# The Fourier step of a gMLP and Fourier block folded by token t and 256 - t, with a list of overflowing experts split in four and the end of the mixture-of-experts stage rearranged

## What is computed

```python
# first block, second half: mixture of experts on t = norm(x)
scores = sigmoid(t @ w_router); eidx = top 8 of 64 experts (from the 4 best of 8 groups)
routed = sum over chosen e of gate[e] * ((silu(t @ w_eg[e]) * (t @ w_eu[e])) @ w_ed[e])
x = x + gate2 * (routed + shared)

# second block, first layer ("ab"), done once for the tokens x and once for 256 context tokens ctx
z = h @ w_in                                   # h = norm(x) or norm(ctx), 256 x 1024
u, v, g_a, x_b, g_b = split(z)                 # each 512 wide
y_a = u * spatial(layer_norm(v)) * silu(g_a)
xb = x_b.reshape(B, 256, 4, 128)
f = real(fft2(xb, axes=(tokens, channels), norm='ortho'))   # 256 tokens, 4 groups of 128 channels
y_b = f * silu(g_b)
x = x + gate * (concat([y_a, y_b]) @ w_out)
# second layer ("c"): window attention over x with keys and values of ctx, final norm
```

## Time and profile before

| | us |
|---|---|
| median of 3 runs (lowest, highest) | 1126.29 (1125.88, 1126.87) |
| the profiled execution, its own time | 1125.17 |
| its span in the trace | 1123.4 |
| TensorE busy with matmuls | 1079.4 (96%) |
| VectorE, ScalarE, GpSimd busy | 380.8, 277.2, 52.6 |
| bytes moved | 335.48 MB, mean 299 GB/s |
| mean granted clock of TensorE | 0.992 |

### The profile page before, as it was taken

The page is one execution under the profiler, slowest core; times in us unless marked ns, Lnnn a source line. Parts: engine busy times, 40 slices in busy tenths (PEclk is TensorE's granted clock), DMA queues, the critical chain, the costliest instruction groups (busy, mean ns, idle before and its releaser), DMA issues.

```text
span 1123.4 us, 17394 instructions
## 1 busy us (share of the span) xinstructions
PE 1079.4 (96%) x7070; PEld 746.9 (66%) x7070; DVE 380.8 (34%) x974; ACT 277.2 (25%) x619; POOL 52.6 (5%) x85
## 2 busy tenths in 40 slices
PE   6999999999999899999999999999989999999988
PEld 4786776688756465565556655456458888887567
DVE  1298976432722211112111121211332011342941
ACT  2124135501511112112111111102322111212951
POOL 0000202103000000000000000001000001100001
PEclk9999999999999899999999999999999999999999
DMA  9999387945679999999999999999995334210000
GB/s 385 336 421 421 125 346 317 419 186 188 263 311 385 372 422 420 420 408 422 422 419 422 419 422 421 417 422 418 401 410 216 113 113 151 111 38 1 1 1 38
DMA packets 48560, 335.48 MB, mean 299 GB/s; under 512 B 5440, under 2 KB 6816, under 8 KB 8672
## 3 DMA queue, kind: packets, MB, share of 16 engines
q1 hardware_dynamic: 46080, 329.01, 71.9%
q10 hardware_dynamic: 2176, 3.37, 1.0%
q0 software_dynamic: 224, 1.97, 0.4%
HBM read 333.28 MB, written 1.05 MB: 298 GB/s over the span
## 4 chain that ended last, share of the span: by engine, by line
PE 85%; DMA 7%; DVE 5%; ACT 1%; issue 1%; SPq 0%; DVEq 0%; ACTq 0%
PE bank L1068 13%; PE bank L533 12%; DMA ring<-experts 6%; PE bank L1112 6%; PE bank L1019 5%; PE bank L1208 5%; PE bank L919 5%; PE bank L940 3%; PE bank L450 3%; PE bank L975 3%; PE bank L1300 2%; PE bank L825 2%; PE bank L1258 2%; PE bank L840 2%; PE bank L663 2%; PE bank L599 2%
## 5 line engine op out<-in xcount | busy, mean ns | idle before, releaser
L1068 PE MATMUL bank<-ring,arena 128*32 128x512 f32 (+1 forms) x1120 | 175.4, 599 | 5.2 <-DMA ring<-experts 5.1
L533 PE MATMUL bank<-hT,ring 128*128 128x256 f32 x608 | 134.0, 380 | 0.7 <-ACT hT L1494 0.7
L533 PEld LDWEIGHTS bank<-hT,ring 128*128 128x128 f32 x608 | 114.7, 190 | 20.3 <-issue 5.1
L1068 PEld LDWEIGHTS bank<-ring,arena 128*32 128x32 f32 (+1 forms) x1120 | 50.9, 121 | 111.5 <-issue 111.2
L1112 PE MATMUL bank<-ring,arena 128*32 128x512 f32 (+1 forms) x560 | 87.5, 596 | 2.0 <-DMA ring<-experts 1.0
L919 PEld LDWEIGHTS bank<-arena 128*128 128x128 bf16 x1152 | 66.3, 98 | 13.1 <-issue 10.1
L919 PE MATMUL bank<-arena 128*128 128x128 bf16 x1152 | 72.3, 219 | 2.0 <-ACT arena L1660 2.0
L2288 DVE TENSOR_TENSOR yhalf<-bank,yhalf 128x512 fp32r<-128x512 f32 x48 | 33.2, 692 | 93.3 <-ACT yhalf L1697 93.3
L1431 POOL TENSOR_TENSOR hT<-hT 128x256 f32<-128x256 f32 x30 | 21.7, 724 | 842.1 <-ACT hT L1488 840.7
L2275 DVE SCALAR_TENSOR_TENSOR arena<-bank,arena 128x256 f32<-128x256 f32 x24 | 11.6, 484 | 142.3 <-ACT arena L1689 137.7
L1208 PE MATMUL bank<-hT,ring 128*128 128x256 f32 x256 | 56.9, 379 | 0.0
(11 more groups left out here) (379 smaller groups left out, 1443.5 us busy)
## 6 DMA issues: line engine op xcount, KB each, us to landing
ring<-experts SPq DMA_DIRECT2D x188, 1024.0 KB, 13.4
ring<-stream SPq DMA_DIRECT2D x119, 1024.0 KB, 12.2
ring<-experts SPq DMA_DIRECT2D x8, 512.0 KB, 7.7
arena<-consts POOLq DMA_DIRECT2D x1, 1664.0 KB, 12.7
resid<-x SPq DMA_DIRECT2D x1, 1024.0 KB, 5.2
resid<-ctx ACTq DMA_DIRECT2D x1, 1024.0 KB, 10.0
arena<-stream SPq DMA_DIRECT2D x1, 1024.0 KB, 10.1
bias_room<-rpb ACTq DMA_DIRECT2D x2, 438.0 KB, 5.9
```

The lines of the kernel that those rows point to most:

```text
L533: mm = mmul(o[:, 0:n_tok], w[:, k, t * P:(t + 1) * P], hT[:, k, 0:n_tok], start=(k == 0), stop=(k == KT - 1))
L1068: mm = mmul(o[at:at + n_slots, :], xg[:, kk, at:at + n_slots], w[g][:, k, :], start=(kk == 0), stop=(kk == KT - 1))
```

## The change

The Fourier transform over tokens is real, and cosine and sine of token t and 256 - t are equal up to the sign. So VectorE first makes sums and differences of tokens t and 256 - t (`fold_tokens`, three instructions), 128 columns of each; token 0 and token 128 need no partner. The channel step then takes the sums with the cosine and the differences with the sine, each 128 columns instead of 256, and one more matmul with a single stationary column puts token 128 into row 0 of the sine part. The token step has 2 matmuls instead of 4. This is done for the four groups of context rows and the four of main rows. The constant `dft_l` halves. `list_more` is split in four parts, one after each of the units 1 to 4. At the end of the expert stage the first four matmuls of the context keys come ahead of the last scatter, and the groups `ac` are taken in the order 0, 2, 1, 3.

```diff
-C2_WIDTHS = dict(dft_c=256, dft_l=4 * 256, cos2=256, sin2=256, wmask=2 * 512)
+C2_WIDTHS = dict(dft_c=256, dft_l=2 * 256, cos2=256, sin2=256, wmask=2 * 512)
...
+            def channels(o, n):
+                mmul(o[:, 0:P], folds[:, n % 2, 0:P], cc("dft_c", 0, P), start=True, stop=True)
+                mmul(o[:, P:2 * P], folds[:, n % 2, P:2 * P], cc("dft_c", P, 2 * P), start=True, stop=True)
+                return mmul(o[0:1, P:2 * P], folds[:, n % 2, P:P + 1], cc("dft_c", 0, P), start=True, stop=True)
+            def tokens(o, at):
+                mmul(o[:, 0:T], at[:, 0:P], cc("dft_l", 0, T), start=True, stop=False)
+                return mmul(o[:, 0:T], at[:, P:2 * P], cc("dft_l", T, 2 * T), start=False, stop=True)
...
-                    done(pe, ("zc", i))
-                    for t in range(TT):
-                        mm = mmul(o[:, 256 * t:256 * t + 256], z_c(i)[:, P * t:P * t + P], cc("dft_c"), start=True, stop=True)
+                    pe.wait_ge(S("folded_c"), i + 1)
+                    mm = channels(o, i)
...
-            scatter(LAST, last=True)
...
-            context_keys(0, 4)
-            for g in range(4):
+            context_keys(0, 4, range(0, 4))
+            scatter(LAST, last=True)
+            context_keys(0, 4, range(4, KT))
+            for g in (0, 2, 1, 3):
...
             def over_channels(g):
-                done(pe, ("z", g))
+                pe.wait_ge(S("folded"), g + 1)
...
+            def fold_tokens(src, n, tag):
+                to = folds[:, n % 2, :]
+                back = bass.AP(src.tensor, src.offset + 255, [list(src.ap[0]), [-1, P - 1]])
+                v.tensor_copy(bc(to[:, 0:1], [P, 2]), bc(src[:, 0:1], [P, 2]))
+                v.tensor_tensor(to[:, 1:P], src[:, 1:P], back, ALU.add)
+                v.tensor_tensor(to[:, P + 1:2 * P], src[:, 1:P], back, ALU.subtract).then_inc(S(tag), 1)
...
             for m in range(LAST + 1):
                 unit(m)
-                if m == 1:
-                    list_more()
+                list_more(m - 1)
...
-            for g in range(4):
+            for g in (0, 2, 1, 3):
                 t, hf = g // 2, g % 2
                 full(dve, ("ac", g))
```

More of the change, by code:

```diff
@@ L338, in halved, with second_in @@
             return src[0] == "exp" and WHOLE[UNIT_OF[src[1]]][src[2]] == "-"
-        second_in = [S(f"second_in{k}") for k in range(RING)]
+        def second_in(n):
+            return S(f"second_in{n % RING}")
         slabs = []
@@ L1029, in context_step @@
                         pe.wait_ge(S("const2_in"), 32)
-                    done(pe, ("zc", i))
-                    for t in range(TT):
-                        mm = mmul(o[:, 256 * t:256 * t + 256], z_c(i)[:, P * t:P * t + P], cc("dft_c"), start=True, stop=True)
+                    pe.wait_ge(S("folded_c"), i + 1)
+                    mm = channels(o, i)
                 elif kind == "fb":
                     done(pe, ("fac", i))
[L1035 to L1038, removed]
+                    mm = tokens(o, fa_c(i))
                 else:
@@ L1211, in over_channels @@
             def over_channels(g):
[L1212 removed]
+                pe.wait_ge(S("folded"), g + 1)
                 o = open_group(("fa", g), 5 + g % 2)
[L1214 to L1216 removed]
+                close_group(channels(o, g), ("fa", g))
             def over_tokens(g):
@@ L1220, in over_tokens @@
                 o = open_group(("fb", g), 0 if g % 2 else 7)
[L1221 to L1226, removed]
+                close_group(tokens(o, fa[:, g % 2, :]), ("fb", g))
             def over_chunk(h):
@@ L2224, in context_out @@
                     ada(3)
+                elif kind == "z" and i < 4:
+                    done(dve, ("zc", i))
+                    if i >= 2:
+                        full(dve, ("fac", i - 2))
+                    fold_tokens(z_c(i), i, "folded_c")
                 elif kind == "sum":
@@ L2292, in unit, with largest @@
                     context_moments()
[L2294 to L2302, removed]
+            def largest(ms):
+                for m in ms:
                     link(v.max(klist[:, 8 * m:8 * m + 8], keys))
@@ L2387, in _ @@
                                 ALU.subtract, ALU.mult).then_inc(S("v_norm"), 1)
+            for g in range(4):
+                done(dve, ("z", g))
+                if g >= 2:
+                    full(dve, ("fa", g - 2))
+                fold_tokens(zT[:, 12 + g, 0:T], g, "folded")
             def fourier(g):
```

68 lines of the change are left out of this document (42 added, 26 removed).

## The result

The changed kernel took 1118.49 us in the median of three runs (1117.03 to 1118.75), against 1126.29 before: a ratio of 0.9932 (95% interval 0.9916 to 0.9947), 7.8 us less. Forecast were 1114.3 us and a range up to 1118.4, so this median lies 0.1 us above the range. Two later series of five runs, each beside the kernel before on one chip, gave 1115.96 (ratio 0.9912, 0.9899 to 0.9924) and 1117.37 us (0.9926, 0.9913 to 0.994), both inside the range; on which side of its edge a median of so few runs falls is chance. All 13 runs of it have a median of 1117.35, all 42 runs of the kernel before 1125.82: 8.5 us.

What follows compares the result with a forecast made beforehand. A full stream of slabs was taken to bound the expert stage, TensorE alone the main rows. Terms 4.0 + 3.7 + 4.3 = 12.0 us off the profiled 1125.17 gave 1113.2, plus 1.1 for the median: 1114.3 us, range 1111.3 to 1118.4.

Steps and rivals of the forecast that it cites:

- Stall: Unit 2: TensorE's 3.91 us wait for VectorE and the half clock behind it, 7.0 us together, go away.
- unit 3's wait for its slab: Expert stage: TensorE reaches unit 3's half 1 early, at 379.8, and waits 3.0 us for a slab landing at 382.8.
- tail without idle time: End of expert stage: context keys between L1112 and the last scatter, with at most 0.5 us idle.
- gap of 1.47: End of expert stage: TensorE idles 1.47 us before the sums of squares L493, which start at 832.96.
- cheap folds on VectorE: Context and main rows: each fold takes VectorE 0.6 us, hidden behind at least one more tile of matmuls; costs nothing.
- Term A: Expert stage: 4.0 us arrives of the 11.3 us TensorE saves; the rest turns into waits for slabs.
- large hole: Slab stream at 382 to 387 us, 143 GB/s: closes, making the whole stream behind it 3.3 us earlier.
- second hole: Four microseconds of slab stream at 346 GB/s, where SyncE waits for TensorE; closes too, giving 0.7 us.
- fall of the clock expected in unit 3: Unit 3, behind the 3.0 us slab wait: clock falls, losing some 1.9 us, covered by TensorE's lead over the stream.
- Term B: End of expert stage, keys ahead of the scatter and order 0, 2, 1, 3: 3.7 us, 1.9 of them the clock.
- Term C: Main rows, all on the chain: four groups at 1.07 us each, 4.3 us; bounds 4.0 to 5.1.
- such a gap did not lower the clock: Sums of squares: full clock after 1.47 us idle, since gaps of 1.51 and 1.69 us had been harmless.

Runs made afterwards that it cites:

- ctx_twice: Changed kernel with each folded channel step and token step of the context rows issued twice; expert stage 505.3 us, against 503.43 in the changed kernel.
- only_fold: Kernel before with only the folded Fourier step, in context and main rows; 1122.23 us, ratio 0.9973 (0.9964 to 0.9982).
- third_full: Changed kernel with the channel step's third matmul at all 128 stationary columns, written to unused columns; main rows 81.22 us against 82.35.
- third_none: Changed kernel without the one-column third matmul of the channel step; main rows 80.32 us against 82.35.

## Why the prediction was off

**The direction and the places were right.** Stall, unit 3's wait for its slab (3.0 forecast, 2.81), closed hole, tail without idle time, gap of 1.47 (1.48), cheap folds on VectorE: all there.

**Term A, 4.0 forecast, 3.1 measured.** The large hole gave 3.25 of its 3.3. The step that failed is "it closes too", said of the second hole: of its 0.7 us next to nothing came, by the landings of the slabs. ctx_twice shows that this hole depends on TensorE's lateness, but 1.07 us less of it is too little. The stage varies by some 1 us without a change, so this miss is hardly larger than its noise. The fall of the clock expected in unit 3 did not come in this profile, and cost nothing where it came in others (see below).

**Term B, 3.7 forecast, 4.0 measured.** Right in mechanism. The slab `cin` 0 landed 3.5 us behind the start of the last down half and not 4.0, so the scatter started hardly later than before and the transposes 1.6 us earlier, not 1.1: that is the surplus, and it was luck. The 1.9 for the clock is 1.7, and not a constant of the kernel before: at the same gap of 2.52 us only_fold kept full clock, so the sum took one execution's fall for the kernel's.

**Term C, 4.3 forecast, 3.1 measured: the step that failed.** "[...] the one with a single stationary column streams the same 128 columns: 0.66." The price of moving columns was right (third_full) and the token step too. What was missing is the change of the stationary's width, 3 x 0.10 us per group. In place of 0.66 us the runs showed 0.95 for the channel step, with 0.66 again once the third matmul had all 128 columns. It could have been read from the trace of before: there, behind L1079, whose stationary has 64 columns, the 16 matmuls that take 3.62 us elsewhere take 3.72.

```profile
491.63 0.21 PE L1079 MATMUL bank<-arena 128*64 128x3 bf16 x4
491.77 3.72 PE L1025 MATMUL bank<-ring,hT 128*128 128x256 f32 x16
```

L1079 is bf16, but the type is not the reason. Between float32 matmul records of 256 columns in that trace, at full clock, the next one starts 0.22 us later where both have 128 stationary columns. It starts 0.31 us later in each of 18 places where 32 columns follow 128, and in each of 9 where 128 follow 32.

**What the sum left out: 2.0 us in the last attention**, the largest miss in the profiled execution, in a part which the diff does not touch: 1.6 for a fall of the clock behind a gap of 1.69 us that had been harmless before, and 0.4 for the pause of VectorE. The fall was put at nothing because one profile had none. 12.0 - 0.9 + 0.3 - 1.2 - 2.0 = 8.2. Without the fall the forecast would have been 2.2 us too low, with it 3.8 in the profiled execution.

**The rule "such a gap did not lower the clock" failed as a rule.** Over the 17 profiles, counting the falls behind a gap of one kind:

| gap of TensorE | falls |
|---|---|
| 1.7 us near 17 | 17 of 17 |
| 1.2 us near 177 | 8 of 17 |
| 1.5 us ahead of the sums of squares | 0 of 13 |
| 1.7 us in the last attention | 4 of 17 |
| 2.5 us ahead of the sums of squares | 3 of 4 |
| 2.5 to 3.5 us at unit 3's half 1 | 4 of 11 |
| 3.9 to 4.8 us in unit 2 | 4 of 4 |
| 1.4 us near 287 | 0 of 17 |
| none, near 145 | 17 of 17 |

Two gaps of 1.7 us, one always followed by a fall and one seldom: the length alone doesn't tell. Nor is a gap needed. Near 145 us the clock fell in every profile, with no idle time of TensorE in the 30 us before it; what TensorE did just before were L797's matmuls of a single moving column. In the kernel before (the third row is a window, its clock the third number from the end):

```profile
141.57 3.67 PE L797 MATMUL bank<-ones,arena 96*128 96x1 f32 x32
145.13 5.37 PE L806 MATMUL bank<-arena,ones 96*96 96x512 f32 x8
147.00:149.00 2.00, 2.00 (x3) 0.51 (x2) 0.98 (x2) 0.92 (x2) 0.00 (x0) 0.50 0.95 377
```

I expected a fall in unit 3; the longest gap there, 3.51 us in third_none, had none. In the four profiles where it fell the stage is no longer than in the others (502.97 to 503.93 us, against 502.89 to 504.20): it is covered, as forecast.

The fall near 177 goes with a first gate/up half at 316.3 us in the mean, against 313.7 without. Not all of these 2.6 us are its own: the low stretch near 145 is twice as long in ten of the profiles, and all eight falls near 177 are among these ten. The half starts at 313.3 to 313.7 us where the stretch near 145 is short (7 profiles) and at 314.1 where it is long and no fall follows near 177 (2). With a fall there it starts at 315.7 to 316.3 (6), and at 317.1 where that fall lasts twice as long too (2). So a fall near 177 costs 1.9 or 3.0 us. Whether it is more frequent in the changed program (8 of 13 profiles with at least two of its parts, 0 of 4 of the others) or by chance these runs don't tell. The kernel before has more falls in some executions than in others too: the mean granted clock of 39 of its runs goes from 0.987 to 0.994, with the lowest in its longest run (1129.91 us) and the highest in eight of 1123.5 to 1124.5 us.

## What to carry to other kernels

Price a matmul by its moving columns only where the stationary keeps its width; at each change look for a longer first matmul behind it, and rather load 128 columns for nothing than one. Work in a stretch that a full stream paces counts by the holes it closes, and a hole whose cause is only made smaller may stay (0.7 us forecast for the second, next to nothing measured). A fall of the clock read from one execution is a draw: put it into the sum with a chance, and where a gap is near one that has fallen, take two or three microseconds into the range for what the change doesn't touch.

## What the runs showed of the hardware

- A one-column stationary of 128 rows cost 0.51 us per 128 moving columns of f32 in its surroundings, a full one 0.22: its load (0.09 us) began with the matmul and not under the one ahead, and so did the next load. In the kernel before, a float32 record of 256 columns held up its follower for 0.31 us in place of 0.22 where the stationary went from 128 columns to 32 or back.
- TensorE's clock fell to half behind a gap of 1.2 us in 8 of 17 profiles, behind one of 1.7 us in 17 of 17 and behind another of 1.7 us in 4 of 17, and stayed at full behind one of 3.5 us in unit 3. It fell in 17 of 17 near 145 us with no gap at all, behind matmuls of one moving column. A fall cost 1.6 us in the last attention, 1.7 in the sums of squares and 1.9 or 3.0 near 177.
- A pause of 0.3 to 0.5 us of VectorE moved from one instruction to another when four instructions were added ahead of it (one execution).
